# A ten-layer fp32 model on one core: TensorE's weight steps half as long, the sparse stage's key projection ahead of its value projection, and a new order of steps on every engine

## The reference

```python
for i in range(4):                                            # first block
    x = x + 0.5 * swiglu(rmsnorm(x, ffn1_norm[i]), ffn1_w_gu[i], ffn1_w_down[i])
    x = x + mixer(i)(rmsnorm(x, mix_norm[i]))                 # gdn, sb, dsa, gdn
    x = x + 0.5 * swiglu(rmsnorm(x, ffn2_norm[i]), ffn2_w_gu[i], ffn2_w_down[i])
x = rmsnorm(x, final_norm)
for l in range(2):                                            # second block
    x = layer_norm(DEEPNORM_ALPHA * x + mixer_sublayer(x, ...), ln1_g[l], ln1_b[l])
    x = layer_norm(DEEPNORM_ALPHA * x + square(relu(x @ w_ff1[l])) @ w_ff2[l], ln2_g[l], ln2_b[l])
```

## Time and profile before

| | |
|---|---|
| timed, median of 3 runs | 2890.73 us (2890.49 to 2891.34) |
| profiled execution, first to last instruction (span) | 2888.2 us |
| PE, PEld, DVE, ACT, POOL busy | 2850.4, 2416.6, 1794.7, 1577.3, 451.5 us |
| DMA | 574.90 MB, mean 199 GB/s |
| mean granted TensorE clock | 0.997 |

### The profile page before, as it was taken

How to read it: one execution, slowest core, us unless ns; L and a number is a source line. 1 busy time by engine, 2 the same in 40 slices (tenths; PEclk the granted TensorE clock), 3 DMA queues, 4 the chain that set the end, 5 groups by cost and what they waited for, 6 DMA issues and landing times. The chain is left out here.

```text
span 2888.2 us, 35966 instructions
## 1 busy us (share of the span) xinstructions
PE 2850.4 (99%) x14255; PEld 2416.6 (84%) x14255; DVE 1794.7 (62%) x2190; ACT 1577.3 (55%) x1982; POOL 451.5 (16%) x700
## 2 busy tenths in 40 slices
PE   9999999999999999999999999999999999999998
PEld 7889888888988888878888898888888888888887
DVE  5558666565666556466556487566675665775664
ACT  5458754544554454565444387644566463566462
POOL 1203512021002112041202107121000020000020
PEclk9999999999999999999999999999999999999999
DMA  8764277686548677537767653486645686645694
GB/s 277 233 192 144 78 217 241 194 247 214 173 153 245 214 229 237 181 117 226 227 207 242 200 160 117 136 248 211 196 147 175 209 284 220 194 146 176 217 280 158
DMA packets 397047, 574.90 MB, mean 199 GB/s; under 512 B 20016, under 2 KB 248624, under 8 KB 396880
## 3 DMA queue, kind: packets, MB, share of 16 engines
q1 hardware_dynamic: 372624, 508.62, 55.9%
q0 software_dynamic: 23680, 62.95, 7.1%
q10 hardware_dynamic: 576, 1.05, 0.1%
HBM read 540.03 MB, written 32.51 MB: 198 GB/s over the span
## 5 line engine op out<-in xcount | busy, mean ns | idle before, releaser
L656 DVE TENSOR_TENSOR lo<-raw,hi 128x2048 fp32r<-128x2048 f32 (+3 forms) x473 | 1050.5, 2234 | 453.7 <-ACT hi L638 453.5
L638 ACT ACTIVATE hi<-raw 128x2048 fp32r<-128x2048 f32 (+2 forms) x487 | 907.2, 1871 | 753.8 <-DMA raw<-in_ffn_w_gu 261.8
L430 PE MATMUL ps<-hi,xh 128*128 128x512 f32 (+1 forms) x2208 | 866.5, 392 | 9.5 <-DVE lo L656 7.0
L432 PE MATMUL ps<-hi,xl 128*128 128x512 f32 (+1 forms) x2208 | 859.6, 389 | 0.0
L431 PE MATMUL ps<-lo,xh 128*128 128x512 f32 (+1 forms) x2208 | 858.9, 389 | 0.0
L430 PEld LDWEIGHTS ps<-hi,xh 128*128 128x128 f32 x2208 | 415.7, 188 | 96.3 <-DVE lo L656 11.9
L432 PEld LDWEIGHTS ps<-hi,xl 128*128 128x128 f32 x2208 | 415.4, 188 | 86.0
L431 PEld LDWEIGHTS ps<-lo,xh 128*128 128x128 f32 x2208 | 415.9, 188 | 83.9 <-issue 0.5
L430 PE MATMUL ps<-hi,hhh 128*128 128x512 f32 x704 | 274.6, 390 | 0.0
L432 PE MATMUL ps<-hi,hhl 128*128 128x512 f32 x704 | 273.9, 389 | 0.0
L431 PE MATMUL ps<-lo,hhh 128*128 128x512 f32 x704 | 273.9, 389 | 0.0
(11 more groups left out here) (440 smaller groups left out, 3397.3 us busy)
## 6 DMA issues: line engine op xcount, KB each, us to landing
raw<-in_ffn_w_gu SPq DMA_DIRECT2D x348, 512.0 KB, 4.9
raw<-in_ffn_w_down SPq DMA_DIRECT2D x80, 1024.0 KB, 5.1
raw<-in_w_ff SPq DMA_DIRECT2D x64, 1024.0 KB, 5.6
raw<-in_w_in SPq DMA_DIRECT2D x60, 1024.0 KB, 5.3
raw<-in_gdn_w_in SPq DMA_DIRECT2D x32, 1024.0 KB, 5.6
turned<-hhf POOLq DMA_DIRECT2D x88, 256.0 KB, 4.7
hhr<-turned POOLq DMA_DIRECT2D x352, 64.0 KB, 4.0
raw<-in_sb_w_in SPq DMA_DIRECT2D x12, 1024.0 KB, 5.1
```

The source lines that it names most:

```text
L430: e.matmul(o, a1, r1, start=kk == 0, stop=False)
L432: i = e.matmul(o, a2, r1, start=False, stop=kk == kts - 1)
L638: k.e.activation(k.m.hi[q % RING][:, 0:n], k.m.raw[q % RING][:, 0:n], ACT.Copy).then_inc(*k.up("act_piece_hi", ("hi", q)))
L656: k.e.tensor_tensor(m.lo[i][:, 0:n], m.raw[i][:, 0:n], m.hi[i][:, 0:n].bitcast(F32), ALU.subtract).then_inc(*k.up("dve_piece_lo", ("split" ...
```

## The change

What the diff does, in four parts.

1. TensorE's row pieces yield after each block of 128 rows (L438), and column pieces after each column tile: twice as many steps `W`, each half as long. The matmuls and their order inside a piece are the same. On the other engines a piece has as many steps as before.
2. In the sparse stage `uk` streams ahead of `uv`, and attention's first scores no longer wait for the values; the products with the values do (`v_ready`).
3. `vector_rope_both` turns both row tiles in six operations, so that 24 rotary operations and two copies fewer are done on VectorE.
4. All strings of steps, of every stage and engine, are new.

```diff
@@ Plan.dsa @@
         self.rows(("uq", g), t["dsa_w_uq"][0], 0, 1024, 3)
+        self.rows(("uk", g), t["dsa_w_uk"][0], 0, 768, 2)
         self.rows(("uv", g), t["dsa_w_uv"][0], 0, 1024, 2)
-        self.rows(("uk", g), t["dsa_w_uk"][0], 0, 768, 2)
@@ a row piece, TensorE @@
-        if len(ts) == 2 and (j % 2 or half == 2) and j < cnt - 1:
+        if j < cnt - 1:
             yield
@@ a column piece, TensorE @@
-        if k0 == 4:
-            k.close(b)
-        yield
+            if k0 == 4 and q == cnt - 1:
+                k.close(b)
+            yield
@@ one line of a table, of some 100 @@
-W W x1 W x1 W W gla W W W W W W decays W W W W W W W decays decays W W W W W gla W decays decays W gla gmlp W gla gmlp
+W W moba W W W W W W W x1 W W x1 gmlp W W W gla W W W W W W W W W W W W W W W W W W decays W W W W W gmlp W gmlp gmlp
@@ tensor_attention @@
-def tensor_attention(k, g, r, qT, kT, v, heads, *ready):
+def tensor_attention(k, g, r, qT, kT, v, heads, v_ready, *ready):
...
             k.wait_ge("pT.s", g, h)
+            k.wait_ge(*v_ready)
             e.matmul(b.ps[:, 0:256], v[:, 0, h * P:(h + 1) * P], pb[h % 2][:, 0:256], start=True, stop=False)
@@ new @@
+def vector_rope_both(k, v, turns, half, tmp, *done):
+
+    e, n = k.e, v.shape[2]
+    cb, sb = (turns[:, :, c:c + half].unsqueeze(2).to_broadcast([P, 2, n, half]) for c in (0, half))
+    x1, x2 = v[:, :, :, 0:half], v[:, :, :, half:2 * half]
+    k.settle("dve_rope")
+    e.tensor_tensor(tmp[:, 0], x1, cb, ALU.mult).then_inc(*k.up("dve_rope"))
+    e.tensor_tensor(tmp[:, 1], x2, sb, ALU.mult).then_inc(*k.up("dve_rope"))
+    e.tensor_tensor(tmp[:, 2], x2, cb, ALU.mult).then_inc(*k.up("dve_rope"))
+    e.tensor_tensor(tmp[:, 3], x1, sb, ALU.mult).then_inc(*k.up("dve_rope"))
+    k.settle("dve_rope")
+    e.tensor_tensor(x1, tmp[:, 0], tmp[:, 1], ALU.subtract).then_inc(*k.up("dve_rope"))
+    e.tensor_tensor(x2, tmp[:, 2], tmp[:, 3], ALU.add).then_inc(*k.up("dve_rope", *done))
@@ the sparse stage, VectorE @@
-        for t in range(2):
-            q = rope[t]
-            vector_rope(k, r["A4"][:, t, :].rearrange("p (h d) -> p h d", h=8), q[:, 0:16], q[:, 16:32], 16, rt_[:, :, :, :],
-                        *([("q.r", g)] if t else []))
-            yield
+        vector_rope_both(k, r["A4"].rearrange("p t (h d) -> p t h d", h=8), rope[:, :, 0:32], 16, rt_, ("q.r", g))
+        yield
```

More of the change, by code:

```diff
@@ L475, in tensor_cols @@
     pieces = plan.of[pid]
-    steps = [tensor_col_piece(k, plan, pid, piece, xh, xl, ready) for piece in pieces]
+    steps = [(tensor_col_piece(k, plan, pid, piece, xh, xl, ready), piece[2]) for piece in pieces]
     for _ in range(2):
-        for step in steps[:first]:
-            next(step)
-            yield
-    for step in steps[first:]:
-        for _ in range(2):
+        for step, cnt in steps[:first]:
+            for _ in range(cnt):
+                next(step)
+                yield
+    for step, cnt in steps[first:]:
+        for _ in range(2 * cnt):
             next(step)
@@ L1243 @@
+gates W W c1 c3 c1 W W E W W E W W E kT nk nq E nq nq E W W E W kT sv Z nq rows W W nq rows rows nq c2 c0 c3 c1 c0 c2
+gates c3 W Z rows W gates c1 W gate a0 a0 W a0 a0 W a1 a0 a1 a0 W a1 a1 W W a1 W a1 W W W W next
 """
 GDN_DVE = """
-x1 clear rbc W W W E E gates W W gates E gates W W gates E W W gates gates W W E c2 c0 nk nk nk nk E c0 nk c3 W W
-nk c2 c1 c3 c1 W W W W inv E E gates W W E W W nq nq nq E E W W nq E W W nq nq qk qk inv c1 c2 c0 qk c3 c0 c0 c2 c1
-c0 c2 c1 a0 a0 c2 c3 a0 c3 c1 a0 a1 a0 a1 c3 a0 qk a1 a0 a1 a1 a1 a1 out W W W W W W W W W W W W out next W W out W
@@ L1290, in pieces @@
         keys = tensor_cols(k, plan, ("k", g), m.xh, m.xl, ready, first=2)
-        for _ in range(4):
+        for _ in range(8):
             yield next(keys)
@@ L1302, in pieces @@
             for s in range(2):
-                for _ in range(2):
+                for _ in range(8 if half and s else 4):
                     next(o[s])
@@ L2138, in dsa_room @@
              kix=v["A2"][:, 0:2, :].rearrange("p a (b c) -> p a b c", b=2), kix2=v["A2"][:, 2:4, :],
-             rope=[m.const[:, C_ROPE + 48 * t:C_ROPE + 48 * (t + 1)] for t in range(2)])
+             rope=m.const[:, C_ROPE:C_ROPE + 96].rearrange("p (t c) -> p t c", t=2))
     return v
 DSA_PE = """
-turn_q normq W normq x1 W W turn_q W W normk W W normq W W W W normk W normk turn_q normk W W index_q W normk index_q
-index index index index index W W W turn_q W turn_k index attention attention attention attention attention attention
@@ L2494 @@
[L2494 to L2497 removed]
+x1 W x1 W W W W lr W W W W decays W decays W W W decays W W W decays decays W gla W gla gla W angles W W gla gv W W W
@@ L2498 @@
+W gla W gla gla angles W W gla gla W W W gmlp W gla gmlp clear moba gmlp moba W gla gmlp decays W gla gmlp decays W
+gla W gmlp gla moba W W W gmlp W gla gla moba gla gmlp W W W attention W attention W y W W gmlp attention y W norm
+attention W W W W gmlp y W W W W attention W W W W attention attention decays W W W W y W attention y W W W W W W yT W
+W y yT W W W W out decays W W norm W next out next W norm W
 """
```

170 lines of the change are left out of this document (86 added, 84 removed).

## The result

The changed kernel takes 2893.12 us in the median of 20 executions (2890.87 to 2909.93), the kernel before 2891.68 (2890.38 to 2892.97). That is 1.4 us or 0.05% more. The ratio over all executions is 1.0014, with an interval of 1.0007 to 1.002: slower, by less than the 0.2% that I called no change. Either way the time is outside the range that I gave (2874.5 to 2890.5). The ratio is above that of the medians because six of the 20 executions took 6 to 17 us more than the median, as one to four executions of experiments 1, 2, 5, 6, 9 and 10 did by 4 us and more and none of the kernel before; the cause is open. The profiled execution of the changed kernel took 2892.06 us, with a span of 2890.3, 2.1 us over the span before.

The account below looks back on a forecast made before the run. TensorE bounds the kernel (busy 2850.4 of 2888.2 us), leaving idle and low-clock time to win. Terms -3.8 - 2.5 - 2 + 0 + 1 = -7.3, with tenths -7.6, gave 2880.6, plus 2.5: 2883.1 us; range 2874.5 to 2890.5.

Parts of the forecast that it names:

- The deltanet term: Two deltanet stages: a wait moves from `lo_20` to `lo_23`, length unchanged; 0 us, bounds per stage -4.7 to +3.
- a rival, with 5.9 us a stage and a chance of 0.09: Deltanet stages: late `goz` delays the chain, TensorE waits 4.3 us more, clock drops again; 11.8 us, 2894.9; chance 0.09.
- The wait of 4.8 us that I expected for `lo_23`: Deltanet stages: TensorE wants split `lo_23` at 292.3 and waits 4.8 us, in place of 3.1, with the clock falling there.
- The sparse term: Sparse stage: fewer rotary operations, earlier keys and ScalarE's new order bring probabilities earlier; -2.5 us, bounds -5 to +1.
- 1.6 us that I named and did not count: Sparse stage: clock loss possible behind a remaining wait of near 2.9 us before the first probabilities; 1.6 us, left out.
- The mixer2 start: First mixer2 stage's start: the `xl` wait and lower clock go, second row tile's `x` costs 0.3; -3.8 us, bounds -2 to -4.5.
- the others: Small starts: later transposes in both ff2 stages and the first feed-forward remove waits; -2 us, bounds 0 to -2.5.
- the new small waits inside mixer2 for which I added 1 us: Allowance for feed-forward, stick-breaking and inside of mixer2, where gla transposes come later; +1 us, bounds 0 to +10.
- the gla branch's room of 3.8 us: Inside mixer2: time from the start of the later gla transposes to their first use, shrunk from 19 us to 3.8.
- two of the four rivals: Waits only move, clock falls in the sparse stage: 2890.8, chance 0.25; late deltanet chain: 2894.9, chance 0.09.
- "slower": Whole kernel: outcome slower by more than 0.2%, given chance 0.08 as the upper part of the late-deltanet-chain rival.

Follow-up runs that it names:

- experiment 1: Changed kernel with the deltanet stages' four step lists put back to the order of the kernel before; 2885.73 us.
- experiment 2: Changed kernel with `goz` and `gow` moved ahead of the first two qkD products on VectorE in the deltanet stages; 2889.47 us.
- experiment 5: As experiment 2, with the first of GpSimd's five weight splits in each deltanet stage made by VectorE; 2883.86 us.
- experiment 6: Changed kernel with the first of the sparse stage's four GpSimd splits made by VectorE, ScalarE's order kept; 2891.46 us.
- experiment 9: Changed kernel with both the deltanet order of experiment 1 and the sparse-stage order of experiment 3; 2882.63 us.
- experiment 10: As experiment 7, with three short weight steps ahead of q's first two norm sums on TensorE in the deltanet stages; 2880.52 us.
- experiment 7: Changed kernel with the edits of experiment 5 and experiment 3 together; 2880.55 us.
- experiment 3: Changed kernel with ScalarE's `hi`, and so GpSimd's first split, moved behind the indexer's scores in the sparse stage; 2889.56 us.
- experiment 4: Kernel before with only the new order at the first mixer2 start: both halves of `xh` and `xl` ahead of the third weight piece; 2888.91 us.

## Why the prediction was wrong

**The deltanet term was the step that failed.** It said: as TensorE came 1.5 us earlier, the stage ends where it did. VectorE's times in it were right: `lo_20` early (280.2, by my sum 287), `lo_23` at 296.5, `goz` at 305.8. TensorE's were not: it came to `lo_23` at 298.65 and did not wait, instead of at 292.3 with 4.8 us to wait, since it had stood for `sy` at 277 us, so that `goz` to 0.1 us is luck in part. More than that, I then let the end of the stage follow from TensorE's arrival and wrote that the chain behind `goz` has lists of its own. The end follows from `goz`: by the stage's own time ScalarE's copies began 4.9 and 4.75 us later, and the stages were 3.92 and 3.96 us longer. I had this as a rival, with 5.9 us a stage and a chance of 0.09. Its threshold (`goz` later than 303.3) was met by my own estimate of 305.9, so that by my own working it was the likeliest case, and I gave it the least but one. Experiments 1, 2 and 5 show it. That rival's price was too high all the same: the second drop of the clock came in one of the two stages only. The wait of 4.8 us that I expected for `lo_23` did not come: TensorE stood for `sy` at 277 us (3.6) and for q's product at 311 us (3.0) instead.

**The sparse term failed in what it left out.** -2.5 us was forecast, +1.05 measured. VectorE's saving of 2.6 us is real (the rotary sets now take 2.7 us less), and ScalarE could copy the first keys 3.2 us earlier by the stage's own time, but I took each of VectorE's operations at its length in the trace of before. I never asked what GpSimd does in the same moment. ScalarE's new order starts GpSimd's split 4.5 us earlier, 7.5 us by the stage's own time, into the scoring. And I left out the clock, 1.6 us that I named and did not count; it fell twice. With the split behind the scoring the stage is 2.7 to 3.5 us shorter than before (experiments 7, 9 and 3), about what my term said.

The Trainium skill has the rule that I should have looked up ("SBUF — State Buffer", Terms and the section SBUF: two separate sides): VectorE and GpSimd share one pair of ports under an exclusive lock that is held for a whole instruction, and VectorE needs it with two inputs from SBUF, against a GpSimd operation that reads SBUF, or in a two-port mode. The traces agree for two inputs, with 4.33 and 4.49 us for an operation of 0.34 to 0.48 us, beside splits of 4.6 us.

**The starts of stages were right.** The mixer2 start gave 3.91 us (3.8 forecast), the others 3.0 with the last stages (2 forecast); the new small waits inside mixer2 for which I added 1 us did not come, and the gla branch's room of 3.8 us was enough.

**The range was too narrow on the upper side**: it ended at 2890.5, below the median of before, although two of the four rivals ended above that, at 2890.8 and 2894.9. The chances have a slip too: "slower" meant over 2896.5, and the only rival on that side ended at 2894.9, so the 0.08 that I took for it out of that rival's 0.09 had nothing under it.

## What to carry to other kernels

When a step moves, ask of its neighbours on the other engines too: a transfer of work to GpSimd is free only while VectorE does nothing that needs the shared port, so place its long operations beside VectorE's work from PSUM or its searches. When two traces are compared inside a stage, take off by how much each entered it early or late. In a stage that hangs on a chain, follow the chain to the stage's last step before a moved wait on TensorE is counted as gain or loss: what TensorE stands for is often not what sets the end. If an estimate meets a rival's own threshold, that rival is the forecast.

## What the runs showed of the hardware

- VectorE and GpSimd exclude each other by instruction. Beside a split on GpSimd (two inputs from SBUF, 4.6 us) an operation with two SBUF inputs took up to 4.94 us for 0.69, a TENSOR_SCALAR in `goz` up to 5.23 us for 0.48 to 0.64. Operations with an input in PSUM (L1666, 0.69 us) and the searches (MAX8 0.61 us for two, MATCH_REPLACE8 0.41 us) had their usual length beside it, as the timelines of VectorE and GpSimd in the changed kernel have it at two places:

```profile
326.31 4.56 POOL L677 TENSOR_TENSOR lo<-raw,hi 128x2048 fp32r<-128x2048 f32 x1 [15.88 <-ACT hi L639]
326.35 0.69 DVE L1666 SCALAR_TENSOR_TENSOR sy<-ps,sl 128x512 f32<-128x512 f32 x1 [0.57 <-PE ps L617]
...
1254.06 4.63 POOL L677 TENSOR_TENSOR lo<-raw,hi 128x2048 fp32r<-128x2048 f32 x1 [5.10 <-ACT hi L639]
...
1254.20 0.41 DVE L2444 MATCH_REPLACE8 dwk<-st,dsc 128x256 f32<-128x256 f32 x1
...
1254.53 0.61 DVE L2441 MAX8 st<-dwk 128x8 f32<-128x128 f32 x2
```

The other way round, GpSimd's operations of 0.45 us in the inverse took 2.3 to 2.4 us when VectorE made a split (2.3 to 2.6 us).
- A wait that replaces a longer one may cost as much, through the clock, but whether it does differs from execution to execution. It fell to half behind waits of 2.3 to 3.7 us, and stayed up behind others of that length. Behind the 2.3 us for `ats` it stayed up in the kernel before and fell in experiment 4. Behind the wait for L1653 in the changed kernel it stayed up in the first deltanet stage (3.0 us) and fell in the second (2.9 us). Behind 3.3 us in the first experiment's last feed-forward it stayed up. So a difference of 1 to 2 us between two traces is not yet an effect of an edit.
